# Delta-rule inverses on 64x64 diagonal blocks with the output norm spread over them, in a two-layer decoder step

## The reference

```
step(s, q, k, v, g, beta):           # per head, chunk by chunk
    g   = cumsum(log g)
    rel = exp(g_t - g_s) for s <= t, else 0
    m   = eye + strict_lower(k k^T * rel) * beta
    w, u = m^-1 [k * beta * exp(g) | v * beta]
    v_new = u - w s
    o   = (q k^T * rel) v_new + (q * exp(g)) s
    s   = s * exp(g_end) + (k * exp(g_end - g))^T v_new
out = rmsnorm(o) * onorm * silu(z)   # per head, over its 128 values; also for GLA's o
x  += out @ w_out
```

## Time and profile before

| | us |
|---|---|
| median of three runs | 2317.8 (2315.2 to 2318.96) |
| profiled execution, its own time | 2319.15 |
| its span, first to last instruction | 2317.0 |
| TensorE busy | 2227.7 |
| VectorE busy | 1094.4 |
| ScalarE busy | 769.4 |
| mean granted clock of TensorE | 0.984 |

### The profile page before, as it was taken

How to read it: one execution, slowest core, us unless ns; L and a number is a source line. 1 busy time by engine, 2 the same in 40 slices (tenths; PEclk the granted TensorE clock), 3 DMA queues, 4 the chain that set the end, 5 groups by cost and what they waited for, 6 DMA issues and landing times.

```text
span 2317.0 us, 43749 instructions
## 1 busy us (share of the span) xinstructions
PE 2227.7 (96%) x17834; PEld 2158.2 (93%) x17834; DVE 1094.4 (47%) x1620; ACT 769.4 (33%) x1055; POOL 98.2 (4%) x165
## 2 busy tenths in 40 slices
PE   8999999998889899999999999999998999999997
PEld 7999999998778789999999999999996599999996
DVE  5444433774446564444433444433556744444432
ACT  5222222343233443222223222222355633222222
POOL 0000000100012200000000000000003200000000
PEclk9999999998989999999999999999999999999998
DMA  4333233432100033333333333333324323333331
GB/s 134 99 91 91 86 91 88 119 82 56 51 19 1 21 104 94 92 92 92 86 91 89 100 91 91 88 92 87 102 74 151 106 64 93 92 92 92 89 91 53
DMA packets 353646, 197.80 MB, mean 85 GB/s; under 512 B 10054, under 2 KB 348130, under 8 KB 353544
## 3 DMA queue, kind: packets, MB, share of 16 engines
q1 hardware_dynamic: 344640, 172.36, 26.0%
q0 software_dynamic: 6736, 21.97, 3.2%
q10 hardware_dynamic: 2176, 2.15, 0.3%
HBM read 188.52 MB, written 8.05 MB: 85 GB/s over the span
## 4 chain that ended last, share of the span: by engine, by line
PE 66%; DVE 3%; ACT 2%; issue 1%; POOL 0%; DMA 0%; POOLq 0%; ACTq 0%
PE PS L1860 58%; PE PS L1968 5%; PE PS L2345 1%; PE PS L2147 0%; DVE Dm L1502 0%; PE PS L2330 0%; DVE tmp L1730 0%; PE PS L2264 0%; PE PS L2278 0%; DVE skX L1679 0%; POOLq L638 0%; DMA tmp<-q_rows 0%; PE PS L1875 0%; DVE dif L1459 0%; DVE skZ L1711 0%
## 5 line engine op out<-in xcount | busy, mean ns | idle before, releaser
L1860 PE MATMUL PS<-hh,whi 128*128 128x260 f32 x3600 | 732.4, 285 | 3.1 <-DVE hl L1781 1.8
L1860 PE MATMUL PS<-hh,wlo 128*128 128x260 f32 x3600 | 728.4, 284 | 0.0
L1860 PE MATMUL PS<-hl,whi 128*128 128x260 f32 x3600 | 727.6, 284 | 0.0
L1187 DVE TENSOR_TENSOR wlo<-stage,whi 128x1024 fp32r<-128x1024 f32 x337 | 412.2, 1223 | 451.8 <-ACT whi L727 442.0
L1860 PEld LDWEIGHTS PS<-hh,whi 128*128 128x128 f32 x3600 | 559.4, 190 | 6.0 <-DVE small L1326 1.5
L1860 PEld LDWEIGHTS PS<-hh,wlo 128*128 128x128 f32 x3600 | 558.3, 189 | 0.0
L1860 PEld LDWEIGHTS PS<-hl,whi 128*128 128x128 f32 x3600 | 557.0, 189 | 0.0
L727 ACT ACTIVATE whi<-stage 128x1024 fp32r<-128x1024 f32 x337 | 352.8, 1048 | 253.1 <-PE PS L1860 244.9
L1860 PE MATMUL PS<-act_h,whi 128*128 128x260 f32 x1408 | 284.0, 283 | 0.0
L1860 PE MATMUL PS<-act_h,wlo 128*128 128x260 f32 x1408 | 283.1, 282 | 0.0
L1860 PE MATMUL PS<-act_l,whi 128*128 128x260 f32 x1408 | 282.5, 282 | 0.0
(11 more groups left out here) (393 smaller groups left out, 1727.9 us busy)
## 6 DMA issues: line engine op xcount, KB each, us to landing
stage<-in_ffn_w_gate SPq DMA_DIRECT2D x88, 512.0 KB, 3.7
stage<-in_ffn_w_up SPq DMA_DIRECT2D x88, 512.0 KB, 3.8
stage<-in_ffn_w_down SPq DMA_DIRECT2D x64, 512.0 KB, 3.9
stage<-in_w_in_e SPq DMA_DIRECT2D x28, 512.0 KB, 3.8
stage<-in_ffn_w_down SPq DMA_DIRECT2D x32, 384.0 KB, 3.4
stage<-in_w_in_o SPq DMA_DIRECT2D x20, 512.0 KB, 3.6
stage<-in_w_out_e SPq DMA_DIRECT2D x8, 512.0 KB, 3.6
stage<-in_w_out_o SPq DMA_DIRECT2D x8, 512.0 KB, 3.6
```

Of the source, the lines that this page charges most:

```text
L1187: dve.tensor_tensor(wlo[:, slot, :], stage[:, s % STAGE_SLOTS, :], whi[:, slot, :].bitcast(F32), ALU.subtract).then_inc(lo_ready, 1)
L1860: mm = pe.matmul(psum[:, half, :], w, x(k)[:, half * HALF:(half + 1) * HALF], start=first and w is hi and x is rhs_hi, stop=last and w is lo)
```

## The change

- The strict lower matrix of each head is split into its two 64x64 diagonal blocks and the 64x64 block below them (`L21`). `cutB`, `X`, `T1` hold blocks: partitions 0 to 63 one block, 64 to 127 the other, 64 columns per head. Levels 1 to 5 work on blocks only; level 6 joins them.
- Two chunks form a pair p. A group of products runs over (block a, chunk of the pair) in two turns (`TURNS`), so that neighbours use other rows of the array and other banks. `level(p, l)` handles both chunks in one go on ScalarE and VectorE.
- Inputs of all four chunks are made ahead (`gdn_inputs`), VectorE cuts the blocks with masks (`gdn_blocks`), GpSimd only masks q k^T and clears a corner.
- The levels of the two pairs are interleaved; the order of all engines is in the `gdn()` functions. State steps go three at a time.
- w and u are solved before the state is known (`solve`), then `past_values` subtracts.
- The norm is split: GLA's heads one by one between the levels, the samples' columns, and then each chunk's four heads at once after its output. The output projection's first unit waits for one GLA head each for its first four k-tiles, then for all of `o_lo`.
- Where TensorE would wait, it multiplies `ones` by `ident` into a bank that is written over (`idle_products`, and three products ahead of `gb_ddc` in levels 4 to 6 of pair 1).
- `gdn_gates` on VectorE gets 14 small copies that fill `blocks` from `masks`. `turned_e` writes the tails elsewhere and gets one small instruction.
- The gates' silu stands before the samples' keys on ScalarE.

```diff
+                    pool.wait_ge(gb_out, 3 * c + 1)
+                    pool.affine_select(out=qk_rel(c), in_=qk_rel(c), compare_op=ALU.is_ge, fill=0.0, base=0,
+                                       pattern=[[0, HB], [1, P]], channel_multiplier=-1).then_inc(gb_mask, 1)
+                pool.wait_ge(gb_mask, NB)
+                for p in range(2):
+                    pool.wait_ge(gb_t1, 2 * (NTH[p, 2] + 1))
+                    for c in (2 * p, 2 * p + 1):
+                        pool.memset(DTf(c)[C:P, :, 0:C], 0.0).then_inc(gb_zero, 1)
                 pool.wait_ge(gb_sc, NB)
...
@@ -1372,6 +1555,16 @@
                 dve.tensor_copy(small[r, TP:TOK], g[:, TP:TOK]).then_inc(gates, 1)
                 dve.wait_ge(gates, 2)
 
+
+                dve.wait_ge(e_consts, 20)
+                for l in range(6):
+                    for a in range(2):
+                        r = slice(a * C, (a + 1) * C)
+                        link(dve.tensor_copy(blocks[r, l, :], masks[r, l, r]))
+                for a in range(2):
+                    r = slice(a * C, (a + 1) * C)
+                    dve.tensor_copy(blocks[r, 6, :], ident[r, r])
...
# ScalarE
+            def level(p, l):
+
+                act.wait_ge(gb_t1, 2 * (NTH[p, l] + 1))
+                r = slice(C if l == 6 else 0, P)
+                for cc in range(2):
+                    act.activation(T1[r, 2 * p + cc].rearrange("p h s -> p (h s)"), level_bank(p, cc, 0)[r, 0:HB * C],
+                                   ACT.Copy).then_inc(gb_t1c, 1)
...
+            def root(n, dst, psum):
+
+                act.wait_ge(hn_sum, n + 1)
+                act.wait_ge(hn_done, n)
+                link(act.activation(dst, psum, ACT.Ln, scale=1.0 / DV, bias=EPS))
+                act.activation(dst, dst, ACT.Exp, scale=-0.5).then_inc(hn_rn, 1)
...
+            def gdn():
+
+                samples_start()
+                gdn_inputs(0)
+                gates_silu(AR)
+                gates_silu(BZ)
+                act.preload_act_table_set(LN_EXP)
+                samples_keys()
+                gdn_inputs(1)
+                samples_e()
+                gdn_first(0)
+                level(0, 1)
+                gdn_inputs(2)
+                states(0, 1, 2)
+                level(0, 2)
+                gdn_inputs(3)
+                states(3, 4, 5)
+                level(0, 3)
+                gla_squares(0)
+                gdn_first(1)
+                gla_root(0)
+                states(6, 7, 8)
+                level(0, 4)
+                gla_squares(1)
+                level(1, 1)
...
# VectorE
+            def gdn_blocks(c):
+
+                dve.wait_ge(gb_out, 3 * c + 3)
+                if c == 2:
+                    dve.wait_ge(tail_stored, 32)
+                low = X[:, c, 0]
+                dve.tensor_tensor(cutB[:, c], X[:, c, 0:1].to_broadcast([P, 5, HB, C]),
+                                  blocks[:, 1:6, :].rearrange("p l (a s) -> p l a s", a=1).to_broadcast([P, 5, HB, C]),
+                                  ALU.mult)
+                link(dve.tensor_tensor(X[:, c, 1], low, blocks[:, 0:1, :].to_broadcast([P, HB, C]), ALU.mult))
+                dve.tensor_tensor(X[:, c, 1], blocks[:, 6:7, :].to_broadcast([P, HB, C]), X[:, c, 1], ALU.subtract)\
+                   .then_inc(gb_dt0, 1)
+
+            def level(p, l):
+
+                dve.wait_ge(gb_dd, 2 * (NTH[p, l] + 1))
+                for cc in range(2):
+                    c, part = 2 * p + cc, level_bank(p, cc, 1)
+                    both = X[:, c].rearrange("p d h s -> p (d h s)")
+                    if l < 5:
+                        dve.tensor_tensor(both, both, part, ALU.subtract).then_inc(gb_ddc, 1)
+                    elif l == 5:
+                        n = HB * C
+                        dve.tensor_tensor(both[:, 0:n], both[:, 0:n], part[:, 0:n], ALU.subtract)
+                        dve.wait_ge(gb_zero, 2 * p + cc + 1)
+                        for a in range(2):
+                            r = slice(a * C, (a + 1) * C)
+                            last = dve.tensor_tensor(DTf(c)[r, :, r], X[r, c, 1], heads4(part[r, n:2 * n]), ALU.subtract)
+                        last.then_inc(gb_ddc, 1)
+                    else:
+                        dve.tensor_scalar(DTf(c)[0:C, :, C:P], heads4(part[0:C, 0:HB * C]), -1.0, None, ALU.mult)\
+                           .then_inc(gb_ddc, 1)
...
+            def norm_apply(n, y, gain, rn, gate):
+
+                dve.wait_ge(hn_rn, n + 1)
+                link(dve.scalar_tensor_tensor(out=y, in0=y, scalar=col(gain), in1=rn, op0=ALU.mult, op1=ALU.mult))
+                dve.tensor_tensor(y, y, gate, ALU.mult).then_inc(hn_done, 1)
...
+            def gdn():
+
+                samples_start()
+                gdn_inputs(0)
+                gdn_inputs(1, 0)
+                gdn_blocks(1)
+                samples_e()
+                gdn_inputs(2)
+                level(0, 1)
+                states(0, 1, 2)
+                gdn_inputs(3, 2)
+                level(0, 2)
+                gdn_blocks(3)
+                states(3, 4, 5)
+                level(0, 3)
+                states(6, 7, 8)
+                level(0, 4)
+                gla_apply(0)
+                level(1, 1)
+                states(9, 10, 11)
+                level(0, 5)
+                gla_apply(1)
+                gla_low(0)
+                level(1, 2)
+                states(12, 13, 14)
+                level(0, 6)
+                gla_apply(2)
+                gla_low(1)
+                level(1, 3)
+                states(15, 16, 17)
+                key_copies(0)
+                gla_apply(3)
+                gla_low(2)
+                level(1, 4)
+                gla_low(3)
+                key_copies(1)
+                samples_apply()
+                level(1, 5)
+                states(18, 19, 20)
+                samples_low()
+                next_state(0)
+                states(21, 22, 23)
+                level(1, 6)
+                key_copies(2)
+                new_values(1)
+                next_state(1)
+                key_copies(3)
+                chunk_apply(0)
...
# TensorE
+            def level_products(p, l):
+
+                if l == 1:
+                    pe.wait_ge(gb_d0c, 2 * (p + 1))
+                else:
+                    pe.wait_ge(sa_kv, 2 * STATES_BY[p, l])
+                if (p, l) in NORMS_BY:
+                    pe.wait_ge(hn_rn, NORMS_BY[p, l])
+                if l > 1:
+                    if p == 1 and l in (4, 5, 6):
+                        for _ in range(3):
+                            mm1(level_bank(p, 1, 0)[:, 0:P], ones[:], ident[:])
+                    pe.wait_ge(gb_ddc, 2 * (NTH[p, l - 1] + 1))
+                if l == 6:
+                    for cc in range(2):
+                        c = 2 * p + cc
+                        for h in range(HB):
+                            mm = mm1(level_bank(p, cc, 0)[C:P, h * C:(h + 1) * C], L21(c)[:, h, :], X[0:C, c, 0, h, :])
+                    mm.then_inc(gb_t1, 2)
+                    return
+                for tiles in TURNS:
+                    mm = []
+                    for h in range(HB):
+                        for a, cc in tiles:
+                            r, c = slice(a * C, (a + 1) * C), 2 * p + cc
+                            mm.append(mm1(level_bank(p, cc, 0)[r, h * C:(h + 1) * C], cutB[r, c, l - 1, h, :], X[r, c, 0, h, :]))
+                mm[-1].then_inc(gb_t1, 1)
+                mm[-2].then_inc(gb_t1, 1)
+
+            def gla_sum(g):
+
+                pe.wait_ge(hn_sq, 2 * HB + g + 1)
+                for half in range(2):
+                    mm = mm1(pair(0)[:, half, :], ones[:], sqG[:, half * HALF:(half + 1) * HALF])
+                mm.then_inc(hn_sum, 1)
+
+            def samples_sum():
+
+                pe.wait_ge(hn_sq, NORM_E)
+                mm1(banks(0, 1)[:, 0:HB * TS], ones[:], qkS[:].rearrange("p h b -> p (h b)")).then_inc(hn_sum, 1)
+
+            def chunk_sum(c):
+
+                pe.wait_ge(hn_sq, NORM_E + c + 1)
+                mm1(banks(6 + c % 2, 1), ones[:], sqC).then_inc(hn_sum, 1)
+
+            def idle_products(p, n):
+
+                for _ in range(n):
+                    mm1(level_bank(p, 0, 1)[:, 0:P], ones[:], ident[:])
+
+            def level_merge(p, l, *steps):
+
+                if (p, l) in ((0, 1), (0, 2), (1, 4), (1, 5), (1, 6)):
+                    idle_products(p, 2)
+                elif (p, l) == (0, 3):
+                    idle_products(p, 1)
+                pe.wait_ge(gb_t1c, 2 * (NTH[p, l] + 1))
+                if p == 1 and l < 4:
+                    gla_sum(l)
+                elif p == 1 and l == 4:
+                    samples_sum()
+                for j in steps:
+                    update_rows(j)
+                if l == 6:
+                    for cc in range(2):
+                        c = 2 * p + cc
+                        for h in range(HB):
```

(80 more changed lines are left out.)

660 lines of the change are left out of this document (390 added, 270 removed).

## The result

The changed kernel takes 2302.41 us (median of four runs, 2300.12 to 2304.07), the kernel before 2318.38 on the same chip (2315.2 to 2319.33): ratio 0.9933, 95 % interval 0.9917 to 0.9949. The forecast was 2302. The profiled execution took 2303.2 us, with a span of 2301.6. What follows reads where those 16 us came from, because the sum came out right though several of its terms were off.

A forecast was written before the change was run, and what follows sets the result against it. TensorE, 96 % busy, was taken to bound the kernel, with gains only in the mixer stage. The walk's 30.5 us less 8 (clock), 1.5 (switches), 4.4 (gates) and 0.8 (projection) gave 16 less: 2302, range 2284 to 2317.

The forecast's parts named there:

- Passes: Block products on TensorE: two blocks run at once, 0.028 us a pass, bounds 0.014 and 0.056; 1088 passes, 30 us.
- Rival 2: Block products: no packing, passes at 0.056 us, 15 us lost, 2317; chance 0.20 shared with the unhidden norm.
- The walk: Mixer stage, engine queues walked from 637.2: output projection start equal to t = 153 instead of 183.5, 30.5 us less.
- switches: Small tiles to full array on TensorE: 0.13 us each, one on the path for each of 12 levels, 1.5 us.
- the start of the projection: Output projection begins at half clock after idle: 0.8 us more than before.
- The clock: Mixer stage: five half-clock spells of about 3.4 us, each costing half of itself, 8 us; bounds 0 and 45.
- The gates: Fourteen VectorE copies in gdn_gates: 2.7 us onto TensorE's wait plus a 1.7 us half-clock spell, 4.4 us; bounds 0 and 4.5.
- The sum: Whole kernel: 30.5 - 8 - 1.5 - 4.4 - 0.8 = 16 us less, median 2302.
- rival 1: Mixer levels: clock holds and VectorE's queue is shorter than walked; 24 to 34 us less, about 2289; chance 0.25.
- rival 3: Mixer levels: half clock throughout, 21 us lost, 2339; chance 0.10.
- Rival 4: Levels 4 to 6 and tail: norm not hidden, 14 us more, 2316; chance 0.20 shared with the no-packing case.

The follow-up runs named there:

- e5_serial: Changed kernel with products of the same array rows issued one behind the other instead of alternating blocks: 2367.8 us, ratio to before 1.0196 to 1.0224.
- e1: Changed kernel with the gates' fourteen VectorE copies moved to before the last input projection tile: 2300.9 us, ratio to before 0.9904 to 0.9931.
- e4: Changed kernel without the change's idle products of ones by ident: 2305.4 us, ratio to before 0.9930 to 0.9957.
- e6: Changed kernel with 8 full products of ones by ident (16 before level 3) in pair 0's waits: 2296.0 us, ratio to before 0.9891 to 0.9920.
- e11: Changed kernel with same-row products issued one behind the other and pair 0's waits filled with full products of ones by ident: 2350.9 us.
- e7_silu: Changed kernel with the gates' silus and table load moved behind pair 0's level 1 on ScalarE: 2311.1 us, ratio to before 0.9959 to 0.9982.
- e12: Changed kernel with the gates' fourteen copies moved before the last projection tile and eight kvS slots: 2284.5 us, ratio to before 0.9843 to 0.9876.
- e2: Changed kernel with eight kvS slots instead of four: 2285.4 us, ratio to before 0.9837 to 0.9868.
- e3: Changed kernel with block 3's input copies moved behind state steps 3, 4 and 5 on VectorE: 2308.5 us, ratio to before 0.9941 to 0.9968.
- e9_all: Changed kernel with the gates' copies moved earlier, eight kvS slots and block 3's input copies behind the state steps: 2279.7 us, ratio 0.9833 to 0.9877.

## Why the prediction was right

**Passes.** Forecast 0.028 us, measured 0.029; e5_serial shows that it hangs on alternating the blocks. Rival 2 (0.056, issue-bound) is out for this order; 0.058 is what the serial order gets. By the figure that the Trainium skill ("TensorE: Matmul & The Clock Gate", Part 2, step 2) gives for MATMULs that the sequencer's microcode handles, some 62 ns each, 16 passes would need 1.0 us, an estimate. They are issued in 0.46, row after row, so that limit did not apply here.

**The walk.** Without the clock it had the levels' first products at t = 29.0 and the end of level 6 at 104.0, 75.0 us. Measured are 27.1 (671.35 - 644.22) and 108.3, 81.1 us: level by level 11.7, 15.6, 11.5, 11.7, 14.6 and 16.0 against 11.3, 13.7, 10.5, 12.0, 14.2 and 13.3. From there to the end 49 were walked and 54.7 measured (57.6 less the four k-tiles). Together 9.9 us more than the walk; clock, switches and the start of the projection, 8 + 1.5 + 0.8 = 10.3, were to cover that. The sum fits; what each of the three cost inside the levels can't be separated in one trace. Which wait would be longest and who would release it was right: 4.60 before level 3, forecast "about 5", released by ScalarE's kvS copy.

**The clock**, the mis-sized term. I took five half-clock spells, each costing half of itself, 8 us. There were 34 us at half clock, twice as much. What one of them costs is less sure. Over whole stages the changed kernel (34.1, 165.8), e1 (47.8, 170.9), e4 (54.6, 169.4) and e6 (13.7, 159.1) lie on a slope of some 0.3 us of stage per us at half clock, as do e5 and e11 (19.2 for 54.6, 0.35), though e6 and e11 also fill waits. The two pairs with the same instructions give 0.43 and 0.44 for the stretch up to level 2. So it is 0.3 to 0.45, somewhat less than half. That a level is a loop through VectorE and ScalarE, whose part doesn't slow, would explain it; it was not tested by itself. 34 us at that price are 10 to 15, not 8. That the whole came out at 2302 in spite of it is partly luck: more half clock at a lower price, and a walk that can't be checked apart from the clock.

**The gates.** In the changed kernel's trace the mixer starts 7.0 us later, for 4.4. Copies and wait were right (3.07 and +2.4), and the products behind them at half clock cost 1.8 as assumed. Of the other 2.8, 2.2 are there before the gates: the last dense products ahead of the wait begin at 504.56 for 502.34, after 6.8 us at half clock at the block's start (483.2 to 490.0) where the kernel before had 3.4 (484.6 to 488.0). That is not the copies' doing: of the eight other traces with the copies at the gates only e7_silu has those 6.8 us, and the median of their starts is some 5 us behind 637.2. So the term was near what was forecast for the start. For the whole kernel moving the copies away won 1.5 us (e1) and 0.9 (e12 against e2), inside the spread, not the 4.4 "straight onto TensorE's wait".

**The sum.** Start +7.0 and stage -20.6 make -13.6 (forecast +4.4 and -20.2, -15.8). The profiled executions differ by -15.95. The other 2.3 us come in the dense products behind, which the change doesn't touch and which I had at 0; the FFN starts 14.5 earlier, so 0.9 of them lie in the output projection. There the forecast had the sign wrong: I let the projection begin at half clock, 0.8 us more than before, without a row that shows it. It was the kernel before that stood at half clock there (0.50 from 819.1 to 822.5, its projection starting at 820.8); the changed kernel's clock is 1.00 from 803 to 813.

**The other rivals.** The clock didn't hold (rival 1), though its time was within reach by another way: e2_slots ends below its 2289, at 2285.4, with 23.9 us still at half clock. Half clock throughout (rival 3) did not come, but e5_serial is it: 2368. So its chance was not for nothing; what decided it was the alternation of the blocks. Rival 4, the norm not hidden and 14 us more, did not come: pair 0's levels 4 to 6 are 2.8 us longer than walked, 42.3 for 39.5, with 17 us at half clock from level 4 on to their end, and leaving GLA's norm out shortened the stage by 7.0 in the one trace there is.

**What stays open.** What sets the clock within a level. Waits alone don't: e3 has 23.9 us at half clock behind two shorter waits, the changed kernel 3.4 behind a longer one, and e1 has 13.7 us more at half clock in a stage whose work is the same and only starts earlier. Neither does busy time as the trace counts it: 90 % busy in e5, at 0.50. And the same kernel differs from one execution to the next, e9_all by 15 us. I can state the granted clock for each version afterwards, and can't forecast it.

## What to carry to other kernels

When small tiles replace full ones, the time is in the loop between the engines: walk each queue and ask which buffer the last copy waits for. Four more slots of a small buffer gave as much (17 us) as the whole rewrite had (16). Judge an edit of a few us in such a stage by the whole kernel's time and not by the wait that it removes, since half clock in the stage grew by 14 to 21 us in three of these runs (e1, e3, e4). Take several executions before ranking two versions: one median came from executions 15 us apart. And when two versions differ, look first whether the difference lies behind the edit at all. Issue blocks that differ in rows and columns alternately; in the one other order tried the packing was lost.

## Not expected of the hardware

- TensorE at 0.50 granted clock for 116 us on end while 90 % busy, with 64x64 blocks issued one after another, 0.058 us a pass at full clock and 0.107 at half; alternated, the same passes take 0.029 at full clock, and the clock averages 0.90 over the stage.
- A microsecond at half clock costs 0.3 to 0.45 us in this stage: 0.43 and 0.44 where two kernels ran the same instructions.
- Moving two groups of VectorE instructions past each other turned 3.4 us of half clock behind a level's wait into 23.9, in the one trace of each.
